# Two of the four probability tiles of each dilated-attention step turned by VectorE instead of TensorE

## What is computed

```python
for g, (window, dil) in enumerate(((128, 1), (512, 4), (2048, 16))):
    og, lg = dilated_group_attention(qg, kg, vg, dil, window // (2 * dil))
wts = softmax(stack(lses))
branch = sum(wts * stack(outs))
```

## Time and profile before

| | |
|---|---|
| median of 3 runs | 1287.54 us (1287.3 to 1291.17) |
| the profiled execution | 1286.9 us, its span 1285.1 us |
| TensorE busy | 1247.7 us (97%) |
| VectorE busy | 892.4 us (69%) |
| ScalarE busy | 705.5 us (55%) |
| DMA, over the span | 154 GB/s, queue 1 busy for 47% |
| TensorE clock granted | 0.997 of full speed |

### The profile page before, as it was taken

How to read it: one execution, slowest core, us unless ns; L and a number is a source line. 1 busy time by engine, 2 the same in 40 slices (tenths; PEclk the granted TensorE clock), 3 DMA queues, 4 the chain that set the end, 5 groups by cost and what they waited for, 6 DMA issues and landing times.

```text
span 1285.1 us, 19018 instructions
## 1 busy us (share of the span) xinstructions
PE 1247.7 (97%) x7448; PEld 1065.7 (83%) x7448; DVE 892.4 (69%) x1603; ACT 705.5 (55%) x1030; POOL 2.4 (0%) x8
## 2 busy tenths in 40 slices
PE   8999999999999999999999999999999999999997
PEld 7997787778888787877998987888888987888885
DVE  6577996684664746547567998766657998766655
ACT  5735577454467565575536575644444676544442
POOL 0000000000000000000000000000000000000000
PEclk9999999999999999999999999999999999999998
DMA  9444432544643335334353544455654544456560
GB/s 277 148 174 137 164 116 82 165 164 164 206 154 125 120 118 164 99 118 133 115 167 101 166 157 132 161 192 175 215 174 144 160 151 133 145 187 205 184 225 33
DMA packets 147343, 197.61 MB, mean 154 GB/s; under 512 B 4765, under 2 KB 102327, under 8 KB 147255
## 3 DMA queue, kind: packets, MB, share of 16 engines
q1 hardware_dynamic: 147126, 196.35, 47.0%
q0 software_dynamic: 128, 0.04, 0.0%
HBM read 195.33 MB, written 1.05 MB: 153 GB/s over the span
## 4 chain that ended last, share of the span: by engine, by line
PE 78%; DVE 12%; ACT 5%; issue 3%; DMA 0%; DVEq 0%; ACTq 0%
PE bank L504 18%; PE bank L506 17%; PE bank L505 17%; PE bank L1517 9%; PE bank L1518 5%; PE bank L592 4%; DVE w_lo L2193 3%; DVE stat L2213 2%; PE bank L1090 1%; PE bank L804 1%; ACT w_hi L1626 1%; PE bank L1127 1%; DVE stat L2210 1%; DVE arena L2207 1%; PE bank L952 1%
## 5 line engine op out<-in xcount | busy, mean ns | idle before, releaser
L2193 DVE TENSOR_TENSOR w_lo<-w_raw,w_hi 128x2048 fp32r<-128x2048 f32 (+5 forms) x190 | 412.9, 2183 | 125.9 <-ACT w_hi L1626 123.6
L1626 ACT ACTIVATE w_hi<-w_raw 128x2048 fp32r<-128x2048 f32 (+5 forms) x190 | 346.3, 1829 | 224.8 <-PE bank L506 152.0
L504 PE MATMUL bank<-w_hi,r_hi 128*128 128x512 f32 (+3 forms) x536 | 207.8, 388 | 2.6 <-DVE w_lo L2193 2.3
L506 PE MATMUL bank<-w_hi,r_lo 128*128 128x512 f32 (+3 forms) x536 | 204.3, 381 | 0.0
L505 PE MATMUL bank<-w_lo,r_hi 128*128 128x512 f32 (+3 forms) x536 | 204.0, 381 | 0.0
L1517 PE MATMUL bank<-h_both,w_hi 128*128 128x512 f32 x512 | 181.2, 398 | 2.0 <-DVE h_both L2994 2.0
L504 PE MATMUL bank<-w_hi,h_both 128*128 128x512 f32 (+3 forms) x464 | 178.3, 384 | 2.0 <-DVE w_lo L2193 1.1
L506 PE MATMUL bank<-w_hi,h_both 128*128 128x512 f32 (+3 forms) x464 | 174.5, 376 | 0.0
L505 PE MATMUL bank<-w_lo,h_both 128*128 128x512 f32 (+3 forms) x464 | 174.4, 376 | 0.0
L1518 PE MATMUL bank<-h_both,w_lo 128*128 128x256 f32 x512 | 143.6, 280 | 0.0
L504 PE MATMUL bank<-h_both,w_hi 128*128 128x256 f32 x464 | 133.9, 289 | 2.1 <-DVE w_lo L2193 2.1
(11 more groups left out here) (318 smaller groups left out, 1595.3 us busy)
## 6 DMA issues: line engine op xcount, KB each, us to landing
w_raw<-in_mlp_w SPq DMA_DIRECT2D x64, 1024.0 KB, 5.3
w_raw<-in_w_out SPq DMA_DIRECT2D x24, 1024.0 KB, 5.0
w_raw<-in_w_in_c SPq DMA_DIRECT2D x48, 512.0 KB, 4.6
w_raw<-in_w_in_c SPq DMA_DIRECT2D x18, 1024.0 KB, 4.9
w_raw<-in_w_in_a SPq DMA_DIRECT2D x12, 1024.0 KB, 6.5
w_raw<-in_w_in_b SPq DMA_DIRECT2D x12, 1024.0 KB, 5.2
w_raw<-in_w_in SPq DMA_DIRECT2D x8, 1024.0 KB, 5.8
w_raw<-in_w_out SPq DMA_DIRECT2D x8, 512.0 KB, 3.6
```

What stands on the lines that cost most here:

```text
L504: nc.tensor.matmul(o, lhs[0], rhs[0], start=start, stop=False)
L506: return nc.tensor.matmul(o, lhs[1], rhs[0], start=False, stop=stop)
L1626: nc.scalar.activation(w_hi[:, u % SPLIT_SLOTS, 0:kts * n], w_raw[:, u % RAW_SLOTS, 0:kts * n], ACT.Copy).then_inc(w_rounded.sem, w_rounde ...
L2193: v.tensor_tensor(w_lo[:, s, 0:m], w_raw[:, u % RAW_SLOTS, 0:m], w_hi[:, s, 0:m].bitcast(F32), ALU.subtract)\
```

## The change

In a d step TensorE turns only the first two tiles of each head (dilation 1), and ScalarE copies 128x256 instead of 128x512. The tiles of dilations 4 and 16 are written into `probT` by VectorE, in the new function `pair_turn`. Its first instruction turns every 32x32 block of both heads' last 256 columns where it stands; four smaller ones then turn the blocks of dilation 4 that lie beside the diagonal, each 32 partitions by 2x32 numbers, into the neighbouring group of 32 partitions. VectorE does this for step q-1 right after `pair_recip(q)`, and for q = 17 after the tail's loop. The m steps stay as they were.

```diff
--- before.py
+++ after.py
@@ -221,6 +221,7 @@
         every = []
         product_done = Steps("product_done")
         act_read = Steps("act_read")
+        probs_turned = Steps("probs_turned")
         dve_read = Steps("dve_read")
         tiles_read = Steps("tiles_read")
         tiles_scaled = Steps("tiles_scaled")
@@ -448,6 +449,12 @@
                 return (L, "mo") if p == 1 else (L, "o", q)
             return (L, "ao", p // 2) if p % 2 and b else (L, "o", q)
 
+        C_BY_TENSOR = 2
+
+        def c_slots(q):
+
+            return masked if q % 2 == 0 else prob[:, 2:4, :]
+
         def c_slot(q, par):
 
             return masked[:, par, :] if q % 2 == 0 else prob[:, 2 + par, :]
@@ -1096,7 +1103,7 @@
                         for par in range(2):
                             pe.wait_ge(probs_scaled.sem, probs_scaled.at((L, q, par)))
                             pr = c_slot(q, par)
-                            cols = [b * S + k * P for k in range(2) for b in range(NB)] if C_PAIRS[q][0] == "m" else [k * P for k in range(4)]
+                            cols = [b * S + k * P for k in range(2) for b in range(NB)] if C_PAIRS[q][0] == "m" else [k * P for k in range(C_BY_TENSOR)]
                             transposes((L, "t", q, par), C_TURN_BANK[par], [pr[:, c:c + P] for c in cols], act_read)
 
                     def pair_values(q):
@@ -1108,6 +1115,8 @@
                                     pe.wait_ge(values_read.sem, values_read.at((L, "v", p // 4, g, kb)))
                         for par in range(2):
                             pe.wait_ge(act_read.sem, act_read.at((L, "t", q, par)))
+                        if kind == "d":
+                            pe.wait_ge(probs_turned.sem, probs_turned.at((L, q)))
                         ob = C_OUT_BANK
                         if p % 2 == 0 and b == 0:
                             if ob in left:
@@ -1896,7 +1905,8 @@
                         for par in range(2):
                             if q:
                                 act.wait_ge(product_done.sem, product_done.at(c_out_key(L, q - 1)))
-                            evac((L, "t", q, par), probT[:, par, :], bank[C_TURN_BANK[par]][:, :], ahead=0)
+                            n = 512 if C_PAIRS[q][0] == "m" else C_BY_TENSOR * P
+                            evac((L, "t", q, par), probT[:, par, 0:n], bank[C_TURN_BANK[par]][:, 0:n], ahead=0)
 
                     def turn(c, g):
                         for t in range(2):
@@ -2583,6 +2593,20 @@
                                 dve.wait_ge(exp_done.sem, exp_done.at((L, q, par)))
                             v.reciprocal(S_(52 + 2 * sl, n), S_(32 + 4 * sl, n)).then_inc(row_recip.sem, row_recip.next((L, q, par)))
 
+                    def pair_turn(q):
+
+                        if C_PAIRS[q][0] == "m":
+                            return
+                        for par in range(2):
+                            dve.wait_ge(probs_scaled.sem, probs_scaled.at((L, q, par)))
+                        if q:
+                            dve.wait_ge(product_done.sem, product_done.at(c_out_key(L, q - 1)))
+                        link(v.transpose(out=probT[:, :, S:], in_=c_slots(q)[:, :, S:]))
+                        for i in range(4):
+                            j = i ^ 1
+                            ins = v.transpose(out=probT[32 * j:32 * j + 32, :, S + 32 * i:S + 32 * i + 32], in_=c_slots(q)[32 * i:32 * i + 32, :, S + 32 * j:S + 32 * j + 32])
+                        ins.then_inc(probs_turned.sem, probs_turned.next((L, q)))
+
                     def heads_out(j, key, parts=range(3)):
                         weights(key, 0 if j == 3 else SPLIT_SLOTS - 1)
                         if j == 2:
@@ -2602,6 +2626,7 @@
                             weights((L, "s", q, 1), SPLIT_SLOTS)
                             if q:
                                 pair_recip(q)
+                                pair_turn(q - 1)
                             if out:
                                 heads_out(*out, (1, 2))
 
@@ -2629,8 +2654,10 @@
                             heads_out(2, (L, "ao", 2), (0,))
                         pair_max(q)
                         pair_recip(q)
+                        pair_turn(q - 1)
                         if q == C_TAIL + 1:
                             heads_out(2, (L, "ao", 2), (1, 2))
+                    pair_turn(C_TAIL + 3)
                     heads_out(3, (L, "ao", 3))
                 if li < len(LAYERS) - 1:
                     hidden_halves(L, LAYER_NAMES[li + 1], *ln_cols(li + 1))
```

## The result

The changed kernel takes 1305.6 us (median of 4 runs, 1304.18 to 1306.68); the kernel before takes 1288.69 us beside it (4 runs, 1287.3 to 1291.17). The ratio is 1.0125, 95% interval 1.0113 to 1.0137, so about 16 us slower. The forecast said slower, 1292.8 us with 1285 to 1300, and the time lies above that range.

What follows compares the result with a forecast made beforehand. TensorE's list of work bounds the kernel. Stalls of 15.95 us, less 7.7 saved and 3.0 of old slow passages, give +5.3 on the profiled 1286.9, so 1292.2; 0.6 up to the median makes 1292.8, range 1285 to 1300.

Steps and rivals of the forecast that it cites:

- all eight steps named: Values would stall after steps 1, 4, 5, 8, 12, 14, 15 and 17, by 0.1 to 3.6 us each.
- one wait for a split: Behind the last turn, TensorE would wait 1.65 us for the next unit's split, queued after that turn on VectorE.
- The first transposition: VectorE's 512 numbers per partition in each d step, costed at a subtraction's 0.693 us, not a rounding copy's 0.423.
- the other-side rival: In all 16 `pair_turned`, TensorE gets back 0.27 us per transpose, not 0.128: 1288.3 us, not slower; chance 0.13.
- The slope of 10 us per us of D: Some 10 stalls hang on each other, so the result moves by about 10 us for each us of D.
- D: Time of VectorE's turn in each d step: 1.35 us, between 0.86 and 2.15; forecast band 1.2 to 1.75, chance 0.50.
- The four small transpositions: On VectorE in each d step, starting 0.135 us apart, since they don't wait for each other: 0.63 us together.
- My upper end: The turn at 2.15 us: blocks pay filling and draining, four small ones 0.9 us, no longer overlapping well; +13.9 us.
- the dear turn: Rival: VectorE's turn takes 1.9 to 2.15 us, giving 1298.6 to 1301.4 us; chance 0.12.
- the walk: Step by step, TensorE's shifted values against the end of VectorE's reciprocals plus D: stalls of 15.95 us, net +5.3 us.
- The saving per step: TensorE loses 4 of 8 transposes per d step, 0.128 us each: 0.51 us, in two steps 0.26, 7.7 us in all.
- old slow passages: 3.0 us of TensorE's earlier waits and short halts that would fall inside the new stalls and be subtracted.

Runs made afterwards that it cites:

- E1: The changed kernel without VectorE's five transpositions and without the values' wait for them, that part of the computation left out: 1284.87 us, 0.9964 of the kernel before.
- E2: The changed kernel with only the first transposition of each turn, the four small ones left out: 1290.25 us, 1.001 of the kernel before.
- E7: The changed kernel with idle matmuls in front of all eight waits of the values: 1298.17 us, 1.0072 of the kernel before.
- E12: The changed kernel with plain copies in place of the four small transpositions, blocks moved but not turned: 1300.82 us, one execution.
- E8: The changed kernel with the small transpositions written into their own group of 32 partitions instead of the neighbour: 1305.33 us, one execution.
- E4: The changed kernel with 9, 12 and 16 idle matmuls in front of the waits after steps 4, 12 and 15: 1301.2 us, 1.0094 of the kernel before.
- E3: The changed kernel with the turn ahead of the step's maxima and the last unit's split ahead of the last turn: 1294.34 us, 1.0043 of the kernel before.
- E5: The changed kernel with VectorE turning only seven steps, behind the reciprocals, TensorE the others: 1288.13 us, 0.9999 of the kernel before.
- E9: The changed kernel with the turn written to an unused buffer and no wait of the values for it: 1291.78 us, 1.0011 of the kernel before.
- E6: The changed kernel with VectorE turning only twelve steps, ahead of the maxima, TensorE the others: 1286.19 us, 0.9984 of the kernel before.
- E11: E6 with six idle matmuls ahead of the transposes of step 15: 1285.49 us, 0.9965 of the kernel before.

## Why the prediction was wrong

**What held.** The direction (slower, 0.62) and the mechanism: the wait in front of the values takes the place of ScalarE's, in all eight steps named, none in steps 9 to 11, the longest in step 16's `pair_values`, and one wait for a split stands at 593 us (near 580 in the forecast). Which steps stall was read from where VectorE's reciprocals end against TensorE's values, and only one wait, of 0.16 us, stood where none was forecast. The first transposition was costed by the slower of its two rows, 0.69, and took 0.70. The pitch, not the duration, was the price of a removed transpose, which E1 shows: the other-side rival, 0.27 us each, would have made E1 17 us faster and not 4.6. The slope of 10 us per us of D held roughly: from E2 (D of 0.81 us in the mean) to E7 (1.72) the stage goes from +2.9 to +11.3, 9 us per us, and up to 12 if E2's fall of the clock is taken off.

**What failed, by size.**

- **The four small transpositions: 0.63 us forecast, 0.99 found.** The step of the prediction was "since they don't wait for each other they start 0.115 us apart". They start 0.25 us apart. E12 shows that copies of that form don't overlap either, E8 that the step from one group of partitions into the next within an instruction has no part in it; why they don't stays open. My upper end had 0.9 for them, "that then no longer overlap well", and for this term that end was the nearest; D as found, 1.84, lies between the forecast's band (to 1.75) and the dear turn (from 1.9), on which I had put 0.12.
- **The signal's way to TensorE: not in the sum, 0.15 to 0.25 us.** From the end of the last small one to the start of the values. Together D is 1.84 us in the mean instead of 1.35. At the slope of 10 this is +4.9 us (the walk, done again with 1.88, gives +10.9 instead of +5.3).
- **The saving per step: 0.51 forecast, 0.44 found.** Eight transposes take 1.03 us, but the four that are left take 0.58: a step's transposes cost as if 0.13 us went with the group and 0.11 with each. With 0.44 instead of 0.51 that is 1.0 us less saved; at D = 1.88 the walk gives +11.4 instead of +10.9 by it.
- **The clock: no term in the sum.** The earlier trace rows showed 1.00 in the whole stretch, and I carried it over to a kernel that halts for 2 to 4 us. Three falls, at most 4.8 us, of which the steps gave some 2 back in the profile; E4 and E7, which fill the halts and save 4.4 and 7.4 us by the medians, show it, though part of their gain is the earlier start of the values.
- **Two smaller ones.** The stalls as listed add up to 15.9 us, not 15.95, which changes nothing. Of the 3.0 us of old slow passages only 2.0 fell inside the new stalls.

Forecast 1292.8, + 4.9 for D, + 0.5 for the saving, + 2.6 for the clock in the stage by the profile, makes 1300.8. Of the last 4.8 us, 1.15 lie in the runs of before, whose median beside the changed kernel is 1288.69, not 1287.54. For the rest the record has a hint. The profiled execution was the fastest of its four. Their mean granted clocks are 0.991 to 0.993, while those of 52 executions of the kernel before are 0.993 to 0.998, 0.996 in the mean, and those of E7 0.996 and 0.997. A difference of 0.0045 is some 6 us of 1303, a rough estimate, since the clocks are given to 0.001 and a low clock in a halt costs nothing. With it in place of the 2.6 the sum is 1292.8 + 1.15 + 4.9 + 0.5 + 6 = 1305.4, against 1305.6. That closes it, but the agreement to a few tenths is luck, and where in the executions that weren't profiled the clock fell isn't known.

The result stands beyond even the dear turn's 1298.6 to 1301.4. The Trainium skill ("VectorE: DVE Perf Modes", The three transpose paths) has 311 ns for a 128x128 block transposition of 16-bit numbers, which had put D near 1.9 us and the result 11 us slower. That D is close to what was found, but by another way: by that rule the first instruction would take 1.24 us, and the row says 0.70; the rest was in the small ones and the signal. Had I used only the trace, the right reading was the bound that doesn't let the small ones overlap, with a term for the clock, which no row of the kernel before could price.

Two expectations among the experiments missed by the same oversight. For E3 and E5 I looked for the saving once the direct wait was gone, and the next chain took it: scores, maxima, exponentials, reciprocals, scaling. TensorE covers it by some 6 us, and in steps 5, 8, 12 and 15 by less, since VectorE comes late to the maxima there. E9 puts the price of that lateness at 6.9 us for the changed kernel. E1 and E6 gave less than expected too (4.6 us for 7.7, and 2.6 by the medians for 4 to 6), and in E2 the clock fell where it was to stay at 1.00.

## What to carry to other kernels

Before work is moved to an idle engine, read at which moment of the step that engine waits for the bound one, and put it there; the end of the chain that feeds the next step was the dearer of the two places tried (the same twelve turns cost 10.5 us more there). The turns took back some 20.7 us (E1 against the changed kernel) of a saving of 4.6, since the waits pass through VectorE's own queue from step to step: count them along the chain, with the signal's way. Price an operation by a row of its own form, and where only other forms are at hand let the short ones not overlap. A bound engine that must halt can lose its clock as well; idle matmuls in the halts cost nothing here and kept it.

## What was not expected of the hardware

- VectorE's block transposition of 128x512 numbers of 4 bytes takes 0.70 us, as a subtraction of that size does (0.693); one of 32x64 takes 0.236, whether it crosses partition groups or not (E8), a copy of 32x64 0.186 (E12). None of the small ones overlapped with the next: they start 0.25 us apart, where four scalings of 128x256 and 0.35 us each started 0.26 apart, each beside the end of the one before.
- From the end of the last transposition to the start of the values that waited for it, TensorE standing still, it was 0.15 us in six cases and 0.25 in three; with idle matmuls in front (E7) 0.05.
- TensorE's granted clock went to its lower level after halts of 2.24, 3.02 and 4.09 us, and in E6 after one of 1.65; it didn't after the halt of 2.26 us at 592 us of the changed kernel, and did after the same halt, 2.27 us, in E7. So the halt's length alone doesn't decide it. Behind the halts that were filled the clock stayed (E4, E7, E11).
- The clock's fall at 20 to 30 us comes in some executions of the same stretch of code and not in others; 0.83 over 10 us is 1.7 us. The spread of the kernel before goes with the clock: of 52 executions the 13 with a mean granted clock of 0.998 took 1287.0 to 1288.9 us, the 14 with 0.995 took 1288.9 to 1291.5. Whether it is this fall or another one in the executions that weren't profiled isn't shown.
